# A decoder layer on one core: the first modulation made in four pairs, each used at once, with the tokens loaded first

## What is computed

```python
mod = jnp.einsum('bd,de->be', jax.nn.silu(c), w_ada) + b_ada[None, :]
sh1, sc1, gt1, sh2, sc2, gt2 = jnp.split(mod, N_MOD, axis=-1)
h = modulate(rms_norm(x, g_pre1), sh1, sc1)      # x * (1 + scale) + shift
proj = jnp.einsum('bsd,dc->bsc', h, w_in)        # 1024 x 3584
...                                              # retention, short convolution, w_out
h = modulate(rms_norm(x, g_pre2), sh2, sc2)
f = peer_ffn(h, w_q, sub_keys, u_tab, v_tab)     # 16384 one-neuron experts, top 16 of 8 heads
x = x + gt2[:, None, :] * rms_norm(f, g_post2)
```

## Time and profile before

| | before |
|---|---|
| median of 3 runs | 1805.73 us (1805.12 to 1810.96) |
| profiled execution | 1804.45 us |
| its span (first to last instruction) | 1802.6 us |
| PE busy | 1736.1 us, 96% |
| DVE, ACT, POOL busy | 1099.8, 590.5, 1046.5 us |
| mean granted clock of PE | 0.987 |

### The profile page before, as it was taken

One profiled execution on the slowest core, in us unless ns is written; L12 is line 12 of the kernel. 1 busy time (PEld: TensorE's weight loads), 2 busy tenths in 40 slices (PEclk: granted clock), 3 DMA queues, 4 the chain that ended last, 5 costly groups with the idle time before them and its releaser, 6 DMA issues.

```text
span 1802.6 us, 31216 instructions
## 1 busy us (share of the span) xinstructions
PE 1736.1 (96%) x12728; PEld 1698.6 (94%) x12728; DVE 1099.8 (61%) x2191; ACT 590.5 (33%) x760; POOL 1046.5 (58%) x693
## 2 busy tenths in 40 slices
PE   5899999999999999999999999999999999999995
PEld 4799988879999999999999999999999999999995
DVE  4732578467477555757662122224788889888884
ACT  5313155343233323323232222223333333333332
POOL 0241010003777888888888888873677787767621
PEclk9899999999999999999999999999999999999997
DMA  7333369674366666665757666668999999999971
GB/s 281 133 144 118 142 248 359 217 268 130 57 126 138 140 127 140 124 141 108 144 108 165 142 140 133 136 141 290 347 363 376 390 357 368 356 372 371 376 282 48
DMA packets 191926, 385.18 MB, mean 214 GB/s; under 512 B 74328, under 2 KB 132056, under 8 KB 176808
## 3 DMA queue, kind: packets, MB, share of 16 engines
q1 hardware_dynamic: 111432, 306.56, 50.3%
q0 software_dynamic: 80352, 76.65, 19.3%
HBM read 318.44 MB, written 64.19 MB: 212 GB/s over the span
## 4 chain that ended last, share of the span: by engine, by line
PE 60%; DVE 8%; issue 4%; ACT 0%; DVEq 0%
PE ps L1522 30%; PE ps L1542 29%; DVE ul L1712 2%; DVE topi L134 1%; PE ps L1499 1%; DVE top L128 0%; DVE h L222 0%; DVE h L213 0%; DVE h L227 0%; DVE pick L217 0%; DVE pick L234 0%; DVE h L206 0%; DVE qp L1829 0%; DVE h L1852 0%; DVE pos L191 0%
## 5 line engine op out<-in xcount | busy, mean ns | idle before, releaser
L99 POOL DMA_INDIRECT gates_dram<-gate,where x384 | 646.5, 1684 | 271.7 <-DVE where L250 131.2
L1522 PE MATMUL ps<-hl,uh 128*128 128x260 f32 x2048 | 414.2, 283 | 7.6 <-DVE ul L1712 7.6
L1522 PE MATMUL ps<-hh,ul 128*128 128x260 f32 x2048 | 413.9, 284 | 0.0
L1522 PE MATMUL ps<-hh,uh 128*128 128x260 f32 x2048 | 413.4, 283 | 0.0
L1712 DVE TENSOR_TENSOR ul<-us,uh 128x1024 fp32r<-128x1024 f32 x132 | 161.1, 1224 | 364.9 <-issue 287.7
L1542 PE MATMUL ps<-cl,uh 128*128 128x384 f32 (+1 forms) x1024 | 344.7, 337 | 0.7 <-issue 0.7
L1542 PE MATMUL ps<-ch,uh 128*128 128x384 f32 x1024 | 344.1, 336 | 0.0
L1542 PE MATMUL ps<-ch,ul 128*128 128x384 f32 x1024 | 344.1, 336 | 0.0
L1522 PEld LDWEIGHTS ps<-hl,uh 128*128 128x128 f32 x2048 | 316.9, 189 | 8.8 <-DVE ul L1712 8.6
L1522 PEld LDWEIGHTS ps<-hh,ul 128*128 128x128 f32 x2048 | 317.0, 189 | 0.0
L1522 PEld LDWEIGHTS ps<-hh,uh 128*128 128x128 f32 x2048 | 316.1, 189 | 0.0
(11 more groups left out here) (221 smaller groups left out, 2238.1 us busy)
## 6 DMA issues: line engine op xcount, KB each, us to landing
us<-utab SPq DMA_DIRECT2D x128, 512.0 KB
pairs<-vtab SPq DMA_DIRECT2D x62, 1024.0 KB
wr<-w_ada SPq DMA_DIRECT2D x24, 1024.0 KB, 6.1
gates_dram<-blank SPq DMA_DIRECT2D x24, 1024.0 KB, 9.5
ahead_dram<-a SPq DMA_DIRECT2D x128, 192.0 KB
qp<-ahead_dram SPq DMA_DIRECT2D x32, 768.0 KB
gt<-gates_dram SPq DMA_DIRECT2D x32, 768.0 KB
wr<-w_in SPq DMA_DIRECT2D x14, 1024.0 KB, 4.7
```

The costliest lines, as they stand in the source:

```text
L99: nc.gpsimd.indirect_dma_start(out=io["gates"].rearrange("g p c a t -> (g p c a t)").unsqueeze(1), out_offset=bass.IndirectOffsetOnAxis(ap ...
L1522: last = nc.tensor.matmul(out[:, half, :], w, r[:, k, half * TH:(half + 1) * TH], start=(k == 0 and q == 0), stop=(k == KD - 1 and q == 2))
```

## The change

- *Order of loads.* The constants and x come first, x in four transfers of two k each with a semaphore each. The pieces of w_ada come as shift and scale in turn (0, 4, 1, 5, 2, then the first piece of w_in, 6, 3, 7). Four more raw buffers (in `vt`, `ext`, `tg`, `pr`, which are used later) let seven pieces load without a wait. The trigonometric table (into `tg`) and the state wait for what used those places.
- *Norm in front.* ACT squares each quarter of x as it lands, PE sums ahead of any modulation product, mean, root and reciprocal follow before the first low half on DVE and the first high half on ACT.
- *Pairs.* Rows 2p and 2p+1 are the shift and the scale of k = 2p and 2p+1. Their turns go to a bank of their own, and `mod_pair(p)` on DVE makes bias, coefficient and sample columns for these two k. The scaled rows, high and low halves of these k follow at once, woven between the remaining weight halves. The first projection pair begins with k = 0 while rows 5 to 7 are still to be made (`modulation_ahead`).
- *Two products unsplit.* Rows 0 and 4 use the raw piece and the float32 product, so no high and low half is made of them.
- *Buffers of the halves.* Two more pairs of high and low buffers (`first_high`, `first_low`, in the place of `qp`) for the front.
- *Expert stage.* The 17 semaphores of the gathers become 4 used in turn, with counts that go up.

```diff
-    order = [(ADA, n) for n in range(ADA_AT[1])]
+    shift_and_scale = [part * ADA_AT[1] // 2 + n for n in range(ADA_AT[1] // 2) for part in range(2)]
+    order = [(ADA, at) for at in shift_and_scale[:5]] + [(WIN, 0)] + [(ADA, at) for at in shift_and_scale[5:]]
     for group in (0, 1, 2, 3, 5, 6, 4):
-        order += [(WIN, group * 2 + n) for n in range(2)]
+        order += [(WIN, group * 2 + n) for n in range(2) if (group, n) != (0, 0)]
...
+        first = ExitStack()
+        first_high, first_low = (sb(first, name, [P, 2, KD, WC], F32R) for name in ("first_high", "first_low"))
+        first.close()
...
-        w_slot = [sem(f"w_slot{n}") for n in range(NSLOT)]
-        in_x, in_c, in_cst, in_trig, in_state, in_misc = (
-            sem(n) for n in ("in_x", "in_c", "in_cst", "in_trig", "in_state", "in_misc"))
+        def as_weights(buffer):
+            return buffer.rearrange("p a b -> p (a b)")[:, 0:KD * WC].rearrange("p (k c) -> p k c", k=KD)
+        EXTRA = 4
+        raw_buffers = [wr[:, n] for n in range(NSLOT)] + [as_weights(b[:]) for b in (vt, ext, tg, pr)]
+        high_buffers = [wh[:, n] for n in range(2)] + [io["first_high"][:, n] for n in range(2)]
+        low_buffers = [wl[:, n] for n in range(2)] + [io["first_low"][:, n] for n in range(2)]
+        split_buffer, split_before = (2, 3, 1, 0, 2, 3, 1), {4: 0, 5: 1, 6: 2, 7: 6, 8: 3}
+        def raw_slot(n):
+            return n if n < NSLOT + EXTRA else (n - EXTRA - NSLOT) % NSLOT
+        def raw_count(n):
+            return 1 if n < NSLOT + EXTRA else (n - EXTRA - NSLOT) // NSLOT + 2
+        def load_before(n):
+            return n - NSLOT - EXTRA if n < 2 * NSLOT + EXTRA else n - NSLOT
+        def buffer_of(i):
+            return split_buffer[i] if i < len(split_buffer) else i % 2
+        w_slot = [sem(f"w_slot{n}") for n in range(NSLOT + EXTRA)]
+        in_x = [sem(f"in_x{n}") for n in range(KD // 2)]
+        first_ts, first_hs, first_hk, first_hh, first_hl = (
+            sem(n) for n in ("first_ts", "first_hs", "first_hk", "first_hh", "first_hl"))
+        in_c, in_cst, in_trig, in_state, in_misc = (
...
-        SPLIT_ROWS = ROWS_2
+        PAIRS = ROWS_1 // 2
         EARLY_SETS = 12
+        def is_split(row):
+            return row < ROWS_2 and row not in (0, 4)
...
-        ADA_BANKS = (((0, 1), 2, 0), ((7,), 7, WC), ((3,), 2, 0))
+        ADA_BANKS = (((4, 5), 6, 0), ((7,), 7, WC), ((3,), 2, 0))
...
-                load(0)
-                sp.dma_start(x[:], io["xT"]).then_inc(in_x, 16)
+                    sp.dma_start(raw_buffers[raw_slot(n)], w_dram[kind][at]).then_inc(w_slot[raw_slot(n)], 16)
                 sp.dma_start(cst[:], io["consts"]).then_inc(in_cst, 16)
-                for n in range(1, NSLOT):
+                for n in range(KD // 2):
+                    sp.dma_start(x[:, 2 * n:2 * n + 2], io["xT"][:, 2 * n:2 * n + 2]).then_inc(in_x[n], 16)
+                for n in range(NSLOT):
                     load(n)
...
+                        sp.wait_ge(wl_ok, FIRST_IN + 1)
                         sp.dma_start(tg[:], io["trig"]).then_inc(in_trig, 16)
                     if n == ROWS_1 + 6:
+                        sp.wait_ge(mod_mm, ROWS_1)
...
                     bank, col = ADA_BANKS[part][1:]
+                    first = n - ADA_AT[part]
+                    if part == 0:
+                        bank, first = bank + n // 2 % 2, n % 2
+                        if n % 2 == 0:
+                            pe.wait_ge(*((mod_ok, n // 2 - 1) if n >= 4 else (ms_ok, 1)))
                     pe.wait_ge(row_ok, n + 1)
...
+                                    if ahead:
+                                        ahead(k)
                                     pe.wait_ge(*each_k(k))
...
+                pe.wait_ge(in_cst, 16)
+                for k in range(KD):
+                    norm_sums(k, sq_ok, 1 + k // 2)
                 pe.wait_ge(clo_ok, 1)
-                for n in range(ROWS_1):
+                pe.wait_ge(both_ok, 1)
+                ada_product()
+                ada_turn()
+                ada_product()
+                for _ in range(3):
                     ada_product()
-                    if n == 0:
-                        pe.wait_ge(both_ok, 1)
-                    else:
+                    ada_turn()
+                def modulation_ahead(k):
+                    if k == 1:
+                        for _ in range(3):
+                            ada_product()
+                            ada_turn()
+                    if k == 2:
                         ada_turn()
-                    if n == 3:
-                        for k in range(KD):
-                            norm_sums(k, sq_ok, 1)
-                ada_turn()
-                pe.wait_ge(mod_ok, 1)
-                blocks(4, lambda k: (hl_ok, k + 2), together=True)
+                blocks(4, lambda k: (first_hl, k + k // 2 + 2), together=True, ahead=modulation_ahead)
+                pe.wait_ge(mod_ok, PAIRS)
...
-                    act.wait_ge(w_slot[n % NSLOT], 16 * (n // NSLOT + 1))
-                    if i >= 2:
-                        act.wait_ge(*used[i - 2])
-                    nc.scalar.activation(wh[:, i % 2], wr[:, n % NSLOT], ACT.Copy).then_inc(wh_ok, 1)
+                    act.wait_ge(w_slot[raw_slot(n)], 16 * raw_count(n))
+                    if i >= 4:
+                        act.wait_ge(*used[split_before.get(i, i - 2)])
+                    nc.scalar.activation(high_buffers[buffer_of(i)], raw_buffers[raw_slot(n)], ACT.Copy)\
+                        .then_inc(wh_ok, 1)
                 def root(n):
...
+                def high_samples(pair_at):
+                    act.wait_ge(first_ts, pair_at + 1)
+                    some = slice(2 * pair_at, 2 * pair_at + 2)
+                    nc.scalar.activation(hh[:, some, SEQ:T], tsm[:, some], ACT.Copy).then_inc(first_hs, 1)
+                def high_prompt(k):
+                    act.wait_ge(first_hk, k + 1)
+                    nc.scalar.activation(hh[:, k, 0:SEQ], h[:, k, 0:SEQ], ACT.Identity, bias=mod[:, k, 0:1])\
+                        .then_inc(first_hh, 1)
...
+                for n in range(KD // 2):
+                    act.wait_ge(in_x[n], 16)
+                    nc.scalar.activation(mix[:, 2 * n:2 * n + 2], x[:, 2 * n:2 * n + 2], ACT.Square)\
+                        .then_inc(sq_ok, 1)
+                root(1)
                 high(0)
-                act.wait_ge(in_x, 16)
-                nc.scalar.activation(mix[:], x[:], ACT.Square).then_inc(sq_ok, 1)
-                for i in range(1, ROWS_1):
-                    high(i)
-                    copy_rows(1)
-                    if i == ROWS_1 - 2:
-                        root(1)
-                high(IN_AT)
                 copy_rows(1)
-                high_h(1, 0)
+                high(1)
+                high(2)
+                copy_rows(2)
+                high(FIRST_IN)
+                act.wait_ge(in_misc, 16 * 5)
+                high_samples(0)
+                copy_rows(1)
+                high_prompt(0)
+                high(4)
+                high_prompt(1)
+                high(5)
+                copy_rows(1)
+                high(6)
+                high_samples(1)
+                copy_rows(2)
+                high_prompt(2)
+                high_samples(2)
+                copy_rows(1)
+                for k in (3, 4, 5):
+                    high_prompt(k)
+                high_samples(3)
+                for k in (6, 7):
+                    high_prompt(k)
...
+                pool.wait_ge(mod_mm, 5)
...
+                def mod_pair(p):
+                    two = slice(2 * p, 2 * p + 2)
+                    dve.wait_ge(turn_mm, p + 1)
+                    sums = ps[:, 6 + p % 2, 0:4 * (1 + NS)].rearrange("p (c k s) -> p c k s", c=2, k=2)
+                    made = mod[:, 0:2 * KD].rearrange("p (c k) s -> p c k s", c=2)[:, :, two]
+                    bias = bad[:, 0:2 * KD].rearrange("p (c k) -> p c k", c=2)[:, :, two]
+                    nc.vector.tensor_tensor(made, sums, bias.unsqueeze(3).to_broadcast([P, 2, 2, 1 + NS]), ALU.add)\
+                        .then_inc(mod_ok, 1)
+                    dve.wait_ge(mod_ok, p + 1)
+                    link(nc.vector.scalar_tensor_tensor(
+                        co[:, 0, two], mod[:, KD + 2 * p:KD + 2 * p + 2], 1.0,
+                        gain[:, 0, two].unsqueeze(2).to_broadcast([P, 2, 1 + NS]), ALU.add, ALU.mult))
+                    link(nc.vector.tensor_tensor(tsm[:, two], tsm[:, two], co[:, 0, two, 1:1 + NS], ALU.mult))
+                    nc.vector.tensor_tensor(tsm[:, two], tsm[:, two], mod[:, two, 1:1 + NS], ALU.add)\
+                        .then_inc(first_ts, 1)
...
                 dve.wait_ge(in_cst, 16)
                 nc.vector.tensor_tensor(both[:], ident[0:2 * (1 + NS), 0:1 + NS],
                                         ident[0:2 * (1 + NS), 1 + NS:2 * (1 + NS)], ALU.add).then_inc(both_ok, 1)
```

(41 more changed lines are left out.)

100 lines of the change are left out of this document (56 added, 44 removed).

## The result

| | before | after |
|---|---|---|
| median | 1805.42 us (1803.64 to 1810.96, 4 runs) | 1786.76 us (1786.66 to 1788.07, 4 runs) |
| profiled execution | 1804.45 us | 1788.07 us |
| its span | 1802.6 us | 1786.3 us |

The ratio is 0.9889, with a 95% interval from 0.9869 to 0.991. Five more rounds of the same kernel gave 0.9895 (0.9879 to 0.9912), 1786.34 us beside 1806.61 us. The forecast was 1791 us (a gain of 14.5 us); the medians give 18.7 us. The measured median lies just inside the lower edge of the range, the ratio taken on the median of before that the forecast stood on (1805.73 x 0.9889 = 1785.7 us) just outside it. The direction was right and so was the mechanism in the front; the size was too small, and one of the missing terms lies at the very end of the program.

What follows compares the result with a forecast made beforehand. PE, 96% busy, was taken as bound early by waits for DVE's weight halves. The third projection block moves from 71.5 to 57.0 us, so 1805.73 - 14.5 = 1791.2, say 1791 us; range 1786.5 to 1798 us.

Steps and rivals of the forecast that it cites:

- the front: Program start up to PE's third projection block: that block starts at 57.0 instead of 71.5 us, a gain of 14.5 us.
- the ring of four semaphores: Expert stage gathers: four semaphores in place of seventeen, reached in the same order, change no wait; between 0 and 1 us.
- What bounds, and that everything behind follows: PE waits for DVE's low halves early on; later work is event-released, so starting d earlier ends the program d earlier.
- The sums: PE's 32 matmul records summing squares of x, ahead of modulation: end at 15.7 us, some 4 us at half clock.
- Rival 1: PE at half clock through all sums of squares until 21.0 us: gain only 9.2 us, 1796.5 us; chance 0.12.
- Loads: Start of program: x quarters at 5.3 to 9.2 us, weight pieces at least 2.5 us ahead of use; cost nothing.
- Unsplit products: Modulation rows 0 and 4: float32 products of 3.62 instead of 2.0 us on PE, beside DVE's work, cost nothing.
- PE never loses its clock behind 20 us: PE, from 20.3 us on: never rests longer than 2.5 us, so full clock was assumed.
- DVE's small steps: DVE from 20.65 to 53.55 us: four pair steps at 1.05 us and four sample lows, 0.8 us together.
- What is late next: Next w_in piece after the first projection pair: high half 54.6, low half 56.9 us, costing PE 1.3 us.
- The marker: Start of the third projection block on PE: 71.5 us before, 57.0 us after.
- Carrying the sum over to the median: Whole time: median of runs shown, 1805.73 us, 1.3 us above the profiled execution, less 14.5 us gives 1791.2 us.

## Why the prediction was right, and where it was not

- **The step that failed: the ring of four semaphores, put at nothing.** The prediction says that it changes "no wait: between 0 and 1 us". It looked at the waits for the gathers only. The last wait of the program is for GpSimd's drain, and that fell from 8.63 to 6.01 us: 2.6 us, more than the front lacked.
- **The term that was mis-sized: the front.** 14.5 us forecast, 16.1 us between the means of V (15.2 us between the first two traces, with V from 108.6 to 110.1 us before and from 92.6 to 93.4 us after). 14.5 + 1.6 + 2.6 = 18.7 us; 1805.7 less that is 1787.0 us, and 1786.8 us were measured. That these meet so closely is luck: single executions of one kernel lie several us apart.
- **What bounds, and that everything behind follows: right up to the end of the first expert loop.** The table shows it to 0.7 us over 1126. It does not hold at the end of the program.
- **The sums: right.** 15.7 us forecast for their end, 15.87 and 16.25 us measured as S. The bound of 21.0 us was not needed: they ran 8.7 to 10.2 us in the traces with the sums in front and PE at rest before them. Rival 1 did not happen.
- **Loads: right for this kernel.** No high half waited for a DMA in the front, though the last quarter of x came at 10.26 us, not 9.2. The cover is as thin as named: with S 1.7 us earlier it was gone.
- **Unsplit products: right in kind.** 3.62 us on PE, in the shadow of DVE. Row 0's did lie in the reciprocal.
- **PE never loses its clock behind 20 us: wrong.** The rest of 2.9 us (2.5 forecast) was followed by half clock in most traces, and the turn came at 29.0 instead of 27.7 us. From S to V it cost 1.15 us, by the two traces of this kernel. It worked against the gain. The premise, that a rest of 1.6 us leaves the clock up, does not hold in every execution either: in the second trace of before half clock began right behind the same rest of 1.57 us, at 41.9 us.
- **Within the front, too large: DVE's small steps.** A pair step took 0.74 us (29.13 to 29.87), not 1.05: its four operations on 16 to 36 elements follow at 0.21 to 0.23 us, and the row behind the last at 0.09, where I had taken the pitch of the old ones on 64 to 144 elements. A low half of sample columns advances DVE by 0.09 us, not 0.2. Four of each make 1.7 us, and the seven low halves at 2.20 instead of 2.245 us make 0.3. Against that DVE idled 2.1 us in all, where 1.1 were listed (the list adds up to 53.4 us, 0.15 under the stated end). DVE ended at 52.63 instead of 53.55 us.
- **What is late next: right.** PE waited 0.7 us for the low half of the next piece, 1.3 forecast. The marker came near 56.1 instead of 57.0 us. V shows the same gain, 15.2 us instead of 14.5.
- **Carrying the sum over to the median: too narrow.** I set the profiled execution 1.3 us under the median, as it was before. The changed kernel's profiled execution, 1788.07 us, lies 1.3 us above its median. By the two first traces the miss of 4.4 us (1791.2 - 1786.8) is 2.6 us from these two offsets of opposite sign and 1.9 us in the traces (16.4 us between the two profiled times, 14.5 forecast). The 1.9 us are 0.7 in the front, 1.5 for the clock in the stage of v, 0.6 behind it, 3.5 lost in the second loop and 2.6 won by the drain. The clock and the second loop vary between executions of the same program: H from 10.2 to 13.6 us for the changed kernel and from 13.6 to 17.0 us for before, the second loop from 537.4 to 541.0 us. The drain does not vary. The range allowed 1.5 us for such spread.
- **Open.** The medians of before and changed are 18.7 and 20.3 us apart, front and drain together 18.7 us. What is left of the second figure is inside its interval (0.9879 to 0.9912, 16 to 22 us). The mean of V rests on three traces and two.

## What to carry to other kernels

Where one engine's list of work carries a stretch, sum that list from its own rows, operation by operation at the size it will have, and look for what starts it; here 1 us at the start of the list was 1 us at its end. Norm, pairs, buffers and load order paid as a set: one of them alone in the old kernel gave some 1 us in the front, and one of them missing from the new one cost 3.8 to 7.7 us at V (1.6 to 7.4 us in the medians). A part that "changes no wait" needs a look at the end of the program too, where all engines drain: here a ratio known to 3 us could not show 2.6 us that stand in every trace to the nanosecond. And before a gain of 1% is stated to a microsecond, read how far two executions of the same program lie apart, and put that in the range.

## What the runs showed of the hardware

- GpSimd's closing drain took 8627 ns in the three traces of kernels with seventeen semaphores for the gathers and 6013 ns in the eleven with four, and the program ended 0.2 us behind it.
- PE's clock falls and rises at times that move between executions of one program: H was between 10.2 and 20.4 us over the fourteen traces of these kernels, worth 5 to 10 us, and 10.2 and 13.6 us in the two of the changed one. The kernel with row 1 unsplit had V 1.0 to 1.8 us earlier than the changed one, and more half clock behind it took that back.
- Matmuls of zeros raised the clock as others do: sums of 7.26 us behind them, 8.7 to 10.2 us from rest.
- x in four transfers finished 0.5 us later than in one; the first quarter was there 4.3 us sooner.
